# Six modulation chunks scaled on ScalarE and folded on GpSimd, router logits in column halves, 23 homes for expert weights

## What is computed

```python
def first_block(...):
    c_act = jax.nn.silu(c)                               # one row of 1024
    mod = c_act @ w_ada[l] + b_ada[l]                    # 6 x 1024 modulation values
    sh1, sc1, gt1, sh2, sc2, gt2 = jnp.split(mod, N_MOD, axis=-1)
    h = modulate(rms_norm(x, g_mix[l]), sh1, sc1)
    mix = hybrid_mixer(h, positions, w_in[l], ...)       # h @ w_in, two attentions, gates, w_out
    x = x + gt1[:, None, :] * mix
    h = modulate(rms_norm(x, g_ffn[l]), sh2, sc2)
    ffn = hierarchical_moe(h, w_rg[l], b_rg[l], w_re[l], b_re[l], w_gate[l], w_up[l], w_down[l])
    x = x + gt2[:, None, :] * ffn

def hierarchical_moe(h, ...):                            # 4 groups of 8 experts, 2 chosen a token
    g_prob = jax.nn.softmax((t @ w_rg + b_rg), axis=-1)  # 4 logits
    e_logits = (t @ w_re + b_re)                         # 32 logits
    # chosen experts: silu(t @ w_gate) * (t @ w_up) @ w_down, weighted and added
```

## Time and profile before

| | us |
|---|---|
| median of three runs | 1336.87 (1333.65 to 1340.9) |
| profiled execution, its time | 1337.66 |
| its span | 1335.9 |
| TensorE busy | 1234.8 (92%) |
| VectorE, ScalarE, GpSimd busy | 630.2, 464.9, 169.3 |
| chain that ended last | TensorE 78%, DMA 8%, VectorE 5% |

### The profile page before, as it was taken

One profiled execution on the slowest core, in us unless ns is written; L12 is line 12 of the kernel. 1 busy time (PEld: TensorE's weight loads), 2 busy tenths in 40 slices (PEclk: granted clock), 3 DMA queues, 4 the chain that ended last, 5 costly groups with the idle time before them and its releaser, 6 DMA issues.

```text
span 1335.9 us, 17671 instructions
## 1 busy us (share of the span) xinstructions
PE 1234.8 (92%) x6918; PEld 872.2 (65%) x6918; DVE 630.2 (47%) x1141; ACT 464.9 (35%) x840; POOL 169.3 (13%) x134
## 2 busy tenths in 40 slices
PE   4899989999999889998889689999998999999995
PEld 1667556678887655544445258898655788787783
DVE  1654366554444354311111165423554676858555
ACT  3333226542222331111111152113655356564414
POOL 0200010000000000000000200700513017722003
PEclk9899999999999999999999899999999999999998
DMA  9565252013333379999999923322001321113201
GB/s 357 212 203 176 95 196 77 30 48 95 95 98 127 115 278 384 412 412 412 411 412 405 410 103 99 95 79 95 2 1 33 91 83 53 57 49 92 83 31 63
DMA packets 61633, 219.37 MB, mean 164 GB/s; under 512 B 6368, under 2 KB 6760, under 8 KB 61552
## 3 DMA queue, kind: packets, MB, share of 16 engines
q1 hardware_dynamic: 55440, 198.86, 41.1%
q10 hardware_dynamic: 3664, 10.47, 2.0%
q0 software_dynamic: 2448, 8.91, 1.7%
HBM read 203.52 MB, written 14.70 MB: 163 GB/s over the span
## 4 chain that ended last, share of the span: by engine, by line
PE 78%; DMA 8%; DVE 5%; issue 4%; ACT 4%; POOL 1%; SPq 0%; ACTq 0%; DVEq 0%; POOLq 0%
PE ps L646 12%; PE ps L647 12%; PE ps L648 12%; PE ps L933 6%; PE ps L914 4%; PE ps L742 3%; PE ps L954 3%; PE ps L765 3%; PE ps L752 3%; DMA ring<-in_w_moe 2%; PE ps L687 2%; PE ps L689 2%; PE ps L688 2%; PE ps L713 1%; DMA RE<-in_w_moe 1%
## 5 line engine op out<-in xcount | busy, mean ns | idle before, releaser
L1648 DVE TENSOR_TENSOR ring_r<-ring,ring_r 128x1024 fp32r<-128x1024 f32 x115 | 143.7, 1254 | 202.5 <-ACT ring_r L1295 201.7
L1295 ACT ACTIVATE ring_r<-ring 128x1024 fp32r<-128x1024 f32 x116 | 121.2, 1053 | 204.4 <-PE ps L648 166.8
L646 PE MATMUL ps<-RB_r,ring_r 128*128 128x512 f32 x320 | 126.9, 397 | 1.1 <-DVE RH L1694 1.1
L648 PE MATMUL ps<-RB_r,ring_r 128*128 128x512 f32 x320 | 124.6, 389 | 0.0
L646 PE MATMUL ps<-RC_r,ring_r 128*128 128x512 f32 x224 | 90.7, 405 | 5.9 <-POOL RD_r L2441 4.7
L648 PE MATMUL ps<-RC_r,ring_r 128*128 128x512 f32 x224 | 87.3, 390 | 0.0
L647 PE MATMUL ps<-RD_r,ring_r 128*128 128x512 f32 x224 | 87.3, 390 | 0.0
L647 PE MATMUL ps<-RG_r,ring_r 128*128 128x512 f32 x208 | 81.1, 390 | 0.0
L2434 POOL DMA_INDIRECT RC<-expert_rows,small x4 | 3.8, 962 | 551.6 <-POOLq L2429 550.7
L933 PE MATMUL ps<-ring,RH 128*64 128x512 f32 x320 | 71.9, 594 | 0.0
L646 PEld LDWEIGHTS ps<-RB_r,ring_r 128*128 128x128 f32 x320 | 60.1, 188 | 16.7 <-issue 4.5
(11 more groups left out here) (462 smaller groups left out, 2603.3 us busy)
## 6 DMA issues: line engine op xcount, KB each, us to landing
ring<-in_w_moe SPq DMA_DIRECT2D x120, 512.0 KB, 15.6
ring<-in_w_post SPq DMA_DIRECT2D x68, 512.0 KB, 3.6
ring<-in_w_pre SPq DMA_DIRECT2D x48, 512.0 KB, 3.7
RE<-in_w_moe SPq DMA_DIRECT2D x44, 512.0 KB, 16.5
RF<-in_w_moe SPq DMA_DIRECT2D x40, 512.0 KB, 14.6
ring<-in_w_pre SPq DMA_DIRECT2D x16, 1024.0 KB, 7.2
expert_rows<-RD ACTq DMA_DIRECT2D x15, 512.0 KB, 6.9
ring<-in_w_pre SPq DMA_DIRECT2D x3, 2048.0 KB, 17.0
```

The lines of the kernel that those rows point to most:

```text
L646: mm(out, part(m)[:, w], xh(k), start=first and k == 0, stop=False)
L648: ins = mm(out, remainder(m)[:, w], xh(k), start=False, stop=last and k == n_k - 1)
L1295: A(part(m), tile, ACT.Copy).then_inc(w_hi, 1)
L1648: v.tensor_tensor(remainder(m), arrival(m)[2], part(m).bitcast(F32), ALU.subtract).then_inc(w_split, 1)
```

## The change

**Modulation chunks 4 to 9.** TensorE's eight matmuls and VectorE's copy of each go. ScalarE multiplies the chunk's weights in place by c (48 instructions of 128 x 512 in its rounds 1 to 11 and behind them); GpSimd adds the eight parts in three instructions of 128 x 2048, 1024 and 512. The `ada_turn`s stay, for chunks 4 to 7 behind columns 4, 6, 8 and 10, for 8 and 9 behind the V pair. The chunks have the buffers RE (4), RD (5, 7, 9) and ring tiles 4 to 7 (6, 8), and SP loads them by other waits; the load of the latent weights waits for chunk 8 to be folded.

```diff
+                if c == 5:
+                    sp.wait_ge(h_lo, KT)
+                elif c in (4, 6, 10, 11):
+                    sp.wait_ge(ada_full, {4: 2, 6: 4}.get(c, c))
+                elif c >= 7:
+                    sp.wait_ge(ada_ev, c - 1)
...
             for i in range(4, 14):
                 load_tile(i)
-                if i % 2:
+                if i in (4, 5):
+                    load_chunk(i + 1)
+                if i in (9, 11, 13):
                     load_chunk(3 + i // 2)
-            sp.wait_ge(ada_full, 10)
+            sp.wait_ge(ada_ev, 9)
...
-            ada_chunk(4)
             for i in range(2, 12):
                 split_column(PE_S1 + i, M_S1 + i, h)
-                if i % 2:
-                    ada_chunk(4 + i // 2)
-                elif i:
-                    ada_turn(3 + i // 2, 1, 16)
+                if i >= 4 and i % 2 == 0:
+                    ada_turn(2 + i // 2, 1, 16)
...
+            def scale_chunk(c, ks):                       # ScalarE
+                if ks[0] == 0:
+                    act.wait_ge(*chunk_landed(c))
+                for k in ks:
+                    part_k = chunk_tiles(c)[:, :, k * P:(k + 1) * P]
+                    ins = A(part_k, part_k, ACT.Copy, scale=cpad[:, k, 0:1])
+                if ks[-1] == KT - 1:
+                    ins.then_inc(ada_full, 1)
             for i in range(12):
                 hi(i + 2)
+                if i >= 1:
+                    scale_chunk(4 + (i - 1) // 2, range(0, 4) if i % 2 else range(4, KT))
...
-                if i >= 2 and i % 2 == 0:                 # VectorE
-                    ada_out(3 + i // 2)
...
+            def fold_chunk(c):                            # GpSimd
+                x = chunk_tiles(c)
+                pool.wait_ge(ada_full, c + 1)
+                for n in (512, 256):
+                    link(g.tensor_tensor(x[:, :, 0:n], x[:, :, 0:n], x[:, :, n:2 * n], ALU.add))
+                pool.wait_ge(ada_done, 4 * (c - 1))
+                g.tensor_tensor(ada_rows(c).rearrange("p (m j) -> p m j", m=4), x[:, :, 0:P], x[:, :, P:2 * P],
+                                ALU.add).then_inc(ada_ev, 1)
+            fold_chunk(4)
+            pool.wait_ge(ada_ev, 5)
             g.memset(RE[96:128, 0:8:2, :], 0.0)
-            g.memset(RE[0:32, 1:8:2, :], 0.0)
+            link(g.memset(RE[0:32, 1:8:2, :], 0.0))
+            pool.sem_inc(zero_ok, 1)
+            for c in range(5, 10):
+                fold_chunk(c)
```

```diff
-                last = mm(ps[0][0:36, :], w_r[:, k, :], hT(k), start=(k == 0), stop=(k == KT - 1))
+                s = k % 2
+                last = mm(ps[0][64 * s:64 * s + 64, :], w_r[:, k, :], hT(k), start=(k < 2), stop=(k >= KT - 2))
...
-                        last = nc.tensor.transpose(ps[1][:, t * 36:t * 36 + 36], PTB[0:36, 0, t * P:(t + 1) * P],
-                                                   ident[0:36, 0:36])
+                        last = mm(ps[1][:, t * 36:t * 36 + 36], PTB[:, 0, t * P:(t + 1) * P], half_sum, start=True, stop=True)
...
-            v.tensor_copy(PTB[0:36, 0, :], ps[0][0:36, :]).then_inc(heads_sb, 1)
+            v.tensor_copy(PTB[:, 0, :], ps[0][:, :]).then_inc(heads_sb, 1)
```

```diff
-MOE_SLOTS = 20
+MOE_SLOTS = 23
...
+                if i == MOE_SLOTS - 2:
+                    sp.wait_ge(sq_used, ST_H2 + KT)
+                if i == MOE_SLOTS - 1:
+                    sp.wait_ge(acc, PE_H + 8)
                 if i >= MOE_SLOTS:
                     sp.wait_ge(moe_used, i - MOE_SLOTS + 1)
```

More of the change, by code:

```diff
@@ L111, in build @@
         small = sb("small", [P, 256])
-        w_r = sb("w_r", [P, KT, 36])
-        wdt = sb("wdt", [P, KT, 16])
+        w_r = sb("w_r", [P, KT, 64])
+        wdt = w_r[:, :, 36:52]
         iota64 = sb("iota64", [P, SLOTS])
@@ L140, in build @@
         strip_sum = small[:, 180:196]
+        half_sum = small[:, 196:232]
         late_w = small[:, 164:180].rearrange("p (t e) -> p t e", t=TT)
@@ L196, in build @@
         wide_slots = [r.rearrange("p (a d) -> p a d", a=4) for r in (REf, RFf)]
+        extra_slots = [PB[:, :, :].rearrange("p a c -> p (a c)"), SQ[:, :, :].rearrange("p a c -> p (a c)"),
+                       RBf[:, 2704:3728]]
         earlier = OTK[:, 0, 256:256 + (TT - 1) * N_EXP].rearrange("p (t e) -> p t e", t=TT - 1)
@@ L218, in build @@
         w_u = sem("w_u")
-        w_moe = [sem(f"w_moe{n}") for n in range(MOE_SLOTS - 4)]
+        w_moe = [sem(f"w_moe{n}") for n in range(PAIR_TILES + 4)]
         z_out = [sem("z_out0"), sem("z_out1")]
@@ L406, in moe_tile @@
             s = i % MOE_SLOTS
-            return wide_slots[s // 8][:, s % 4, :] if s % 8 < 4 and s < 12 else ring[:, s - 4 if s < 8 else s - 8, :]
+            if s < PAIR_TILES:
+                return ring[:, s, :]
+            if s < PAIR_TILES + 8:
+                return wide_slots[(s - PAIR_TILES) // 4][:, s % 4, :]
+            return extra_slots[s - PAIR_TILES - 8]
         def slot_sem(i):
             s = i % MOE_SLOTS
-            return w_in[s - 4] if 4 <= s < 8 else w_moe[s if s < 4 else s - 4]
+            if s < 4:
+                return w_in[s]
+            return w_moe[s - 4] if s < PAIR_TILES + 8 else (w_u, w_ada[1], w_ada[2])[s - PAIR_TILES - 8]
         def slot_base(i):
-            return 16 * (M_Q2 // 4) if 4 <= i % MOE_SLOTS < 8 else 0
+            s = i % MOE_SLOTS
+            if s < 4:
+                return 16 * (M_Q2 // 4)
+            return (0, 16, 112)[(s >= PAIR_TILES + 8) + (s > PAIR_TILES + 8)]
         def moe_landed(i, n_over=0):
@@ L424, in moe_landed @@
                 return slot_sem(i), 16 * loads + n_over * 16
-            if i - N_FIRST - PAIR_TILES < PAIR_TILES - 4 or i >= N_FIRST + PAIR_TILES + MOE_SLOTS:
+            if i - N_FIRST - PAIR_TILES < MOE_SLOTS - PAIR_TILES or i >= N_FIRST + PAIR_TILES + MOE_SLOTS:
                 return slot_sem(i), slot_base(i) + 16 * loads
@@ L441, in chunk_tiles @@
         def chunk_tiles(c):
-            if c == 2:
-                return RH[:, :, :].rearrange("p (t a) c -> p t (a c)", t=4)
+            if c in (2, 4, 5, 7, 9):
+                return {2: RH, 4: RE}.get(c, RD)[:, :, :].rearrange("p (t a) c -> p t (a c)", t=4)
             a = 8 if c == 1 else 4
@@ L448, in chunk_landed @@
         def chunk_landed(c):
-            if c in (1, 2):
-                return w_ada[c], 16
-            return w_ada[0], (16 if c == 0 else 32 * (c - 2))
+            if c < 4:
+                return w_ada[c % 3], 16 * (c // 3 + 1)
+            return w_ada[c % 3], (16 if c % 3 else 32) + 32 * ((c - 1) // 3)
         Z_BEHIND = 10
@@ L528, in load_chunk @@
                     return
-                sp.wait_ge(ada_full, c)
+                if c == 5:
[4 more added lines that the diff above has]
+                    sp.wait_ge(ada_ev, c - 1)
                 for b in range(2):
                     n = 17 + 3 * (2 * (c - 4) + b)
-                    sp.dma_start(ring[:, 4 + 2 * b:6 + 2 * b, :],
-                                 pre_d[n:n + 2].rearrange("t p d -> p t d")).then_inc(w_ada[0], 16)
+                    sp.dma_start(chunk_tiles(c)[:, 2 * b:2 * b + 2, :],
+                                 pre_d[n:n + 2].rearrange("t p d -> p t d")).then_inc(w_ada[c % 3], 16)
             def load_tile(m):
@@ L728, in attend @@
                 first, last_n = groups[0] * NPU, (groups[-1] + 1) * NPU
+                pe.wait_ge(zero_ok, 2)
                 def place(n):
@@ L817, in _ @@
             split_pair_tok(PE_V[0], M_V, h)
+            ada_turn(8, 1, 16)
             ada_turn(9, 1, 16)
@@ L1332, in _ @@
             act.dma_start(ext_row[:, 255:640], rel_d[:, 0:385]).then_inc(rev_in, 16)
-            act.dma_start(w_r[:, :, :], wr_d).then_inc(w_small, 16)
+            act.dma_start(w_r[:, :, 0:36], wr_d).then_inc(w_small, 16)
             act.dma_start(wdt[:, :, :], wdt_d).then_inc(w_small, 16)
@@ L1364, in _ @@
                     norm(2, ST_KV, 1, 2, lambda k: kvT, lambda k: None, eps1)
+            scale_chunk(9, range(4, KT))
             evict(PE_V[0] + 1, v_dst(PE_V[0] + 1, 1))
@@ L1785, in _ @@
                     dve.sem_inc(rinv_used, 1)
-            ada_out(9)
             evict(PE_V[0], v_dst(PE_V[0], 0))
@@ L2395, in _ @@
                                  pattern=[[1, P]], channel_multiplier=1))
+            g.memset(w_r[:, :, 52:64], 0.0)
+            g.tensor_tensor(half_sum, ident[:, 0:36], ident[:, 64:100], ALU.add)
             pool.sem_inc(consts, 1)
```

2 lines of the change are left out of this document (1 added, 1 removed).

## The result

The changed kernel takes 1346.19 us (median of 9 runs, 1343.33 to 1348.51), the one before, measured beside it, 1337.79 (9 runs): ratio 1.0062, interval 1.005 to 1.0074, so 8.4 us slower. The profiled execution is 1346.26, its span 1344.5. TensorE has 7.8 us less to do than in the earlier trace rows, and the span is 8.6 us longer.

A forecast was written before the change was run, and what follows sets the result against it. TensorE, busy 92% of the span, bounds the first projection, a chain the router, DMA the later expert stage. 1337.66 + 12.8 + 2 - 2.4 - 3.8 = 1346.3, or 1345.5 against the median (chance 0.52); range 1327 to 1354.

The forecast's parts named there:

- Start: Kernel start: two router loads in 2048 runs instead of 256 delay ScalarE's squares; +2 us, bounds 0 and +3.6.
- What goes: First projection: TensorE loses 96 instructions, 11.5 us of busy time; VectorE loses six copies of 0.69, not on its path.
- A sum of 2048: First projection: GpSimd's largest addition in each fold of a modulation chunk takes 4.5 us, bounds 3.8 and 4.7.
- Turns at SBUF: First projection: GpSimd's folds and VectorE's SBUF instructions, angles included, alternate whole instructions; each shuts VectorE out up to 4.5 us.
- Rival B: First projection: GpSimd works beside VectorE after all for these shapes; turns end 6.5 us earlier, time 1326 us; chance 0.22.
- C: First projection: only two-input instructions alternate, the angles' seven scalar ones pass; +7.5 us, time 1340; chance 0.16.
- the walk: First projection, followed in order of each engine's list: TensorE stands 17 us for column 4's eviction; stage ends +12.8 us.
- The rest of the walk: First projection after the eviction of column 4: V pair ends at 153.5, two turns at 155.2 against 142.4, +12.8 us.
- Router: Router stage: product in column halves saves 3.0 us, plain matmuls for transposes cost 0.6; -2.4 us, bounds 0 to -2.7.
- Experts: Expert stage: three more tiles loaded in the DMA's pause end the later stream earlier; -3.8 us, bounds 0 to -3.8.
- rival D: Expert stage: the added homes do nothing, since TensorE sets the stage's end; time 1349 us; chance 0.10.

## Why the prediction was right, and where it was off

The forecast was 1345.5 against the median; 1346.19 was measured, beside a kernel before that was 0.9 over the median that the forecast started from. The mechanism is as forecast. That the sum of the terms (8.6) meets the profiles' (8.6) so closely is luck: the start was 1.0 too high and the first projection 0.4, the router gave 1.0 less, the experts 0.8 more, and 1.1 behind them was not forecast. By its steps:

- **Start.** +2 forecast, +1.0 measured (first square 17.94 to 18.95; 0.9 with the short runs alone; 1.0 given back by long runs). The term was mis-sized: 1792 more runs cost 1.0 us at the first square, 0.6 ns a run and not 2 ns. The 1.3 us that the earlier trace rows leave over 412 GB/s had been put down to short runs alone.
- **What goes.** 96 matmul instructions of `ada_chunk` are gone, as the part-1 counts show (6918 less 96, plus 4 as the four transposes become eight entries: 6826).
- **A sum of 2048.** 4.5 forecast by the slope through the earlier trace rows, 4.61 measured where nothing was in its way.
- **Turns at SBUF.** Held, whole instruction by whole instruction, and for single-input ones too: L1752 has one input and took 4.78. Rivals B and C, each of which let the angles or a part of them pass, fall with that row. That the angles' wait is the cause of the stand is shown by moving them: 9.9 us come back. The angles were forecast to end at 95.7 or so; they ended at 95.90. The eviction was forecast at 96.4 and came at 96.05, the stand at 17 and was 17.0. With the start's 1.0 in the measured times the walk was about 1.3 us too late there.
- **The rest of the walk.** V pair at 153.5 (plus the start's 1.0), measured 153.56; both turns done at 155.2 (plus 1.0), measured 156.3, where the small projections start (156.14). For the kernel before the walk had 142.4 at that place, and the trace has 142.80 (the prediction set its 142.4 beside the V pair's end, one turn earlier). So +12.8 was +12.3, and +12.4 up to the router. Errors stand against each other in it. The walk left out that TensorE comes back at half clock after the stand (from 97 to 102 us at 0.54 it does 2.7 us of full-speed work, so some 2.3 are lost), the 2.4 for the squares, and 0.9 for GpSimd's last sum. Against that it had 3 us of wait for `lo` of tile 13, where 1.3 were measured, and it came to the eviction 1.3 too late.
- **Router.** -2.4 forecast, -1.4 measured (both in the changed kernel and alone). The product took 6.14 us for 8.61, where 5.6 had been forecast; the granted clock around it was 0.51 (0.66 before), and 6.1 is near what the prediction had for half clock. That is 2.5 of the 3.0. Another half microsecond was lost behind it: from the product's end to the first `gate_up` 21.15 us pass for 20.06, 1.1 more where 0.6 had been taken for the transposes. The clock was back at 1.00 from 484 to 494 and fell again: 0.51 from 494 to 500, where the eight matmuls with `ones` took 1.81 for 1.00. It fell before too, but later, in the gather (0.66 from 485 to 490). From 488 to 494 TensorE had been busy for 3.28 of the 6 us. Why it falls earlier was not tried.
- **Experts.** -3.8 forecast, -3.4 measured alone and -4.6 in the changed kernel. The DMA's share stays at 1.03 from 580 to 700 and TensorE's busy time in it rises from 110.7 to 114.0: the stream sets the end, as forecast, and rival D falls. Where the further 1.2 us and the +1.1 after the experts come from was not tried; the modulation part alone has 275.7 us in this stage, 1.4 under before, with the same 20 homes, so it belongs to that part or to scatter.
- **Rival B's time** (1326) would have been too good even with its mechanism: without the long sums altogether the kernel took 1330. Its walk had -6.5 at the end of the turns; there the small projections start at 142.04, with the start's 1.0 taken off 1.8 earlier than before. The walk had no lower clock in it (some 3.8), and of the 6.1 us of waits only 1 us.

## What to carry to other kernels

Before work goes to GpSimd, list what VectorE does in SBUF at that time and who waits behind it in its list: a sum of n elements can hold each such instruction for its whole length, and a chain of ten small ones meets one long instruction after another. What an idle engine takes over is then paid by the busiest one. Where order within 0.1 us decides such a meeting, time a kernel more than a few times before it is believed.

## What the runs showed of the hardware

**What GpSimd's clears block.** Beside its clears VectorE's two-input instructions pass and its single-input ones don't. In the last profile of the angles in rounds 1 and 3 (1335.22 us, rows above), three two-input ones took 0.69 us each from 75.04 on, the first two of them beside a clear that ran from 74.76 to 76.76. Before them a single-input one (0.43 when alone) waited out the other clear. Timeline of VectorE and GpSimd of that run:

```profile
72.75 1.97 POOL L2454 MEMSET RE<- 32x2048 f32 x1
...
73.01 1.99 DVE L1752 TENSOR_SCALAR SB<-SB 128x512 f32<-128x512 f32 x1
...
74.76 2.00 POOL L2455 MEMSET RE<- 32x2048 f32 x1
```

A small size doesn't help: in the changed kernel a single-input instruction on 8 elements (L1827) took 1.07 us beside the clear at 157.07, and a two-input one on 8 elements just ahead of it (L1826) 0.17. Both kinds wait for GpSimd's sums. The Trainium skill (SBUF — State Buffer, section "Who interferes with whom") has this as two rules: an instruction with two SBUF inputs contends only with a GpSimd instruction that reads SBUF, and one in a 2-port mode with any, each held for the whole instruction. The traces agree with the first, and with the second if the single-input ones (0.43 us for 512 elements, where two-input ones take 0.69) run in such a mode, which no view shows.

**A granted clock that falls after a stand.** After 17.0 us without work TensorE had 0.54 for 5 us. In the kernel without the long sums it stood for 3.7 us; from 84.73 to 90.44 its matmuls then start 0.43 us apart (granted clock 0.50, the 1.2 GHz level), and 0.23 apart from there on (2.4 GHz), which costs some 2.9 us. After the two waits of 1.2 us the clock stayed at 1.00. Work taken from TensorE in a stage where it then waits for some us is thus worth less than its busy time.

**The same wait, another time at the low level.** In all fourteen profiles TensorE stands 5.0 us ahead of the first projection. From its first matmul there to the first that is followed at 0.23 us, 3.0 us pass in the kernel before and 2.7 in the changed one, but 5.6 with the router's part alone and 6.1 with the modulation part alone. It is not the price of a part, as the changed kernel has both of these parts and 2.7; what decides it was not tried. 3.4 us at half clock are 1.7 us of time: a stage read from one profile can be off by that much.
